# Moving projection cover from stick-breaking attention into the gated delta rule, with value transposes inside the l2 norm

## The reference

```python
(q_sb, k_sb, v_sb, q_dn, k_dn, v_dn, z_dn, b_dn, a_dn, r_sb, r_dn) = jnp.split(u @ w_in, offsets, axis=-1)
y_sb = stick_breaking_attention(rms(q_sb), rms(k_sb), v_sb) @ w_up_sb        # 8 heads x 64
qkv = silu(causal_depthwise_conv(concat([q_dn, k_dn, v_dn]), w_conv))        # 4 taps, 12 chunks of 128 channels
q_b, k_b = l2_norm(q), l2_norm(k)                                            # per head, 128 wide
o = gated_delta_rule_chunked(q_b, k_b, v_b, g, beta)                         # 4 heads x 128, a triangular solve per chunk
y_dn = (rms_norm(o, g_dn_out) * silu(z_dn)) @ w_up_dn
merged = sigmoid(r_sb) * y_sb + sigmoid(r_dn) * y_dn
```

## Time and profile before

| | |
|---|---|
| median of 3 runs | 1314.07 us (1313.59 to 1314.76) |
| the profiled execution | 1316.56 us, span 1314.8 us |
| TensorE busy | 1261.0 us, 96% of the span |
| VectorE, ScalarE, GpSimd busy | 646.7, 604.9, 61.9 us |
| mean granted TensorE clock | 0.986 of full speed |
| chain that ended last | TensorE 87%, ScalarE 5%, VectorE 4% |

### The profile page before, as it was taken

One profiled execution on the slowest core, in us unless ns is written; L12 is line 12 of the kernel. 1 busy time (PEld: TensorE's weight loads), 2 busy tenths in 40 slices (PEclk: granted clock), 3 DMA queues, 4 the chain that ended last, 5 costly groups with the idle time before them and its releaser, 6 DMA issues.

```text
span 1314.8 us, 18145 instructions
## 1 busy us (share of the span) xinstructions
PE 1261.0 (96%) x6637; PEld 1012.2 (77%) x6637; DVE 646.7 (49%) x927; ACT 604.9 (46%) x1101; POOL 61.9 (5%) x96
## 2 busy tenths in 40 slices
PE   6999999999997999999988999999799999999998
PEld 4778888887775777777767788787578888888887
DVE  4566666664445463665466366563533333332221
ACT  5476666664444455555664434553332222222211
POOL 0000000001110000000202021002000000000000
PEclk8999999999998999999989999999899999999999
DMA  9676777775652233222222110553133333333330
GB/s 312 188 199 183 191 191 191 188 206 149 163 150 56 64 80 81 65 64 81 81 57 65 50 49 26 160 176 96 49 96 96 96 96 98 98 116 109 104 89 25
DMA packets 278036, 152.38 MB, mean 116 GB/s; under 512 B 8005, under 2 KB 273374, under 8 KB 277982
## 3 DMA queue, kind: packets, MB, share of 16 engines
q1 hardware_dynamic: 273758, 149.54, 40.8%
q10 hardware_dynamic: 4224, 2.10, 0.5%
HBM read 145.31 MB, written 6.29 MB: 115 GB/s over the span
## 4 chain that ended last, share of the span: by engine, by line
PE 87%; ACT 5%; DVE 4%; issue 1%; DMA 1%; SPq 0%; ACTq 0%; DVEq 0%
PE tail L1416 12%; PE region L1416 12%; PE region L1417 12%; PE region L1418 12%; PE tail L1418 12%; PE tail L1417 12%; ACT ada_raw L582 2%; PE region L1628 2%; PE region L1434 1%; ACT w_hi L562 1%; PE region L1543 1%; PE region L1614 1%; PE region L1663 1%; PE region L1692 1%; DMA ada_early<-in_w_ada 1%
## 5 line engine op out<-in xcount | busy, mean ns | idle before, releaser
L562 ACT ACTIVATE w_hi<-raw 128x1024 fp32r<-128x1024 f32 (+1 forms) x177 | 197.7, 1117 | 519.6 <-PE tail L1418 275.8
L953 DVE TENSOR_TENSOR w_lo<-raw,w_hi 128x1024 fp32r<-128x1024 f32 (+1 forms) x177 | 229.5, 1297 | 276.2 <-ACT w_hi L562 274.6
L1416 PE MATMUL region<-u_hi,w_hi 128*128 128x512 f32 x656 | 259.2, 395 | 2.6 <-DVE w_lo L953 2.5
L1418 PE MATMUL region<-u_hi,w_lo 128*128 128x512 f32 x656 | 255.4, 389 | 0.0
L1417 PE MATMUL region<-u_lo,w_hi 128*128 128x512 f32 x656 | 255.4, 389 | 0.0
L1416 PEld LDWEIGHTS region<-u_hi,w_hi 128*128 128x128 f32 x656 | 123.1, 188 | 31.4 <-issue 5.0
L1416 PE MATMUL tail<-u_hi,w_hi 128*128 128x512 f32 x344 | 144.4, 420 | 1.9 <-DVE w_lo L953 1.9
L1417 PEld LDWEIGHTS region<-u_lo,w_hi 128*128 128x128 f32 x656 | 123.1, 188 | 27.6 <-issue 2.2
L1418 PEld LDWEIGHTS region<-u_hi,w_lo 128*128 128x128 f32 x656 | 123.1, 188 | 25.5
L1416 PE MATMUL tail<-g_hi,w_hi 128*128 128x512 f32 x352 | 141.7, 403 | 0.0
L1418 PE MATMUL tail<-g_hi,w_lo 128*128 128x512 f32 x352 | 139.2, 395 | 0.0
(11 more groups left out here) (307 smaller groups left out, 1484.6 us busy)
## 6 DMA issues: line engine op xcount, KB each, us to landing
raw<-in_w_ffn_in SPq DMA_DIRECT2D x168, 256.0 KB, 3.3
ada_raw<-in_w_ada SPq DMA_DIRECT2D x56, 512.0 KB, 5.1
raw<-in_w_in SPq DMA_DIRECT2D x90, 256.0 KB, 3.3
raw<-in_w_ffn_out SPq DMA_DIRECT2D x32, 384.0 KB, 4.6
raw<-in_w_ffn_out SPq DMA_DIRECT2D x32, 320.0 KB, 4.0
ada_early<-in_w_ada SPq DMA_DIRECT2D x8, 1024.0 KB, 9.5
gates<-kept_gates SPq DMA_DIRECT2D x16, 256.0 KB, 4.2
raw<-in_w_out SPq DMA_DIRECT2D x16, 256.0 KB, 3.3
```

What stands on the lines that cost most here:

```text
L562: act.activation(w_hi[:, slot % 2, 0:k, :], raw[:, slot, 0:k, :], ACT.Copy).then_inc(hi_ready, 1)
L953: dve.tensor_tensor(w_lo[:, slot % 2, 0:k, :], raw[:, slot, 0:k, :], w_hi[:, slot % 2, 0:k, :].bitcast(f32), ALU.subtract).then_inc(lo_rea ...
L1416: pe.matmul(bank(b), wh, xh, start=start and n == 0, stop=False)
L1418: ins = pe.matmul(bank(b), wl, xh, start=False, stop=stop and n == k - 1)
```

## The change

The order of `MIXED` becomes: ba, twelve conv, four z, sixteen gate. Attention takes three units for each pair and not four. The cover counts change to match: attention gives up 8 chunks for each pair, "silu" (the first l2 round) has 12 chunks, later rounds 8, "prep" 10 and "solved" 5. The first two squares and the first step of cover come ahead of the Silu of v and of the table load in ScalarE's queue. The transposes of v move behind the statistics of rounds 1 and 2, their copies behind the exponentials of those rounds. The four transposes of k go to four PSUM banks in place of two, without a wait for the copies.

```diff
-    + [m for h in range(4) for m in (("conv", 5 + h), ("gate", h))] + [("z", h) for h in range(4)] \
-    + [("gate", g) for g in range(4, 16)]
+    + [("conv", 5 + h) for h in range(4)] + [("z", h) for h in range(4)] + [("gate", g) for g in range(16)]
-FILL_0 = Z_0 + 4
+FILL_0 = Z_0 + 1
-SHADOW = {"keep": 20, "weights": 6, "y": 6}
-FILL = {"l2": 8, "start": 8, "prep": 7, "inv0": 2, "norm": 4, "level": 2, "join": 1, "solve": 2, "solved": 2, "step": 1, "last": 2}
+SHADOW = {"keep": 18, "weights": 3, "y": 3}
+FILL = {"silu": 12, "l2": 8, "start": 8, "prep": 10, "inv0": 2, "norm": 4, "level": 2, "join": 1, "solve": 2, "solved": 5, "step": 1,
+        "last": 2}
-    return PAIR_0 + 4 * p + n
+    return PAIR_0 + 3 * p + n
-            return gate_out if g >= DNH and g % 2 else rstd
+            return gate_out if g % 2 else rstd
# ScalarE, attention
-                mixed(pair_unit(p, 2))
                 act.wait_ge(y_ps, p + 1)
                 act.activation(ysb_hi[:, p, :], region[0][:, 0:S], ACT.Copy).then_inc(y_hi_ready, 1)
-                mixed(pair_unit(p, 3))
+                mixed(pair_unit(p, 2))
# ScalarE, l2 norm
-            act.activation(conv[:, 8:12, :], conv[:, 8:12, :], ACT.Silu).then_inc(dn_silu, 1)
-            act.preload_act_table_set("natural_log_exp_and_others")
...
                 l2_squares(m)
-                if m < DNH - 1:
-                    mixed(Z_0 + 1 + m)
-                else:
-                    fill("l2")
+                fill("l2" if m else "silu")
+                if m == 0:
+                    act.activation(conv[:, 8:12, :], conv[:, 8:12, :], ACT.Silu).then_inc(dn_silu, 1)
+                    act.preload_act_table_set("natural_log_exp_and_others")
...
+                if m in (1, 2):
+                    v_copies(range(2 * m - 2, 2 * m))
             fill("start")
-            for q in range(NB):
-                act.wait_ge(nat_ps, q + 1)
-                act.activation(v_dn[:, q], heads(bank(4 + q % 2)), ACT.Copy).then_inc(nat_v_ready, 1)
# TensorE, l2 norm
+                if m in (1, 2):
+                    v_transposes(range(2 * m - 2, 2 * m))
             fill("start")
...
+            pe.wait_ge(nat_v_ready, NB)
             pe.wait_ge(l2_ready, 8)
             for q in range(NB):
-                if q >= 2:
-                    pe.wait_ge(nat_ready, q - 1)
                 for h in range(DNH):
-                    ins = pe.transpose(bank(2 * (q % 2))[:, h * P:(h + 1) * P], conv[:, 4 + h, q * P:(q + 1) * P],
+                    ins = pe.transpose(bank((0, 2, 4, 5)[q])[:, h * P:(h + 1) * P], conv[:, 4 + h, q * P:(q + 1) * P],
                                        ident[:, :])
```

More of the change, by code:

```diff
@@ L729, in mixed @@
                 else:
-                    stored(act, d if d < DNH + 2 else d - 1)
+                    stored(act, max(d - 1, 0))
                     act.activation(gate_buffer(d)[:, :], b, ACT.Copy).then_inc(proj_ready, 1)
@@ L785, in _, with v_copies @@
                 act.activation(conv[:, L2[r], :], conv[:, L2[r], :], ACT.Silu).then_inc(dn_silu, 1)
-            act.activation(conv[:, 8:12, :], conv[:, 8:12, :], ACT.Silu).then_inc(dn_silu, 1)
-            act.preload_act_table_set("natural_log_exp_and_others")
+            def v_copies(qs):
+                for q in qs:
+                    act.wait_ge(nat_ps, q + 1)
+                    act.activation(v_dn[:, q], heads(bank(4 + q % 2)), ACT.Copy).then_inc(nat_v_ready, 1)
             def l2_squares(m):
@@ L818, in _ @@
                 act.wait_ge(nat_ps, NB + q + 1)
-                act.activation(k_dn[:, q], heads(bank(2 * (q % 2))), ACT.Copy).then_inc(nat_ready, 1)
-            act.wait_ge(proj_ready, 12 + FILL_0)
+                act.activation(k_dn[:, q], heads(bank((0, 2, 4, 5)[q])), ACT.Copy).then_inc(nat_ready, 1)
+            act.wait_ge(proj_ready, 12 + Z_0 + 4)
             act.activation(z_gate[:, :, :], z_gate[:, :, :], ACT.Silu).then_inc(z_silu, 1)
@@ L1224, in _ @@
                 mixed(pair_unit(p, 1))
-                split_lo(DN_IN + pair_unit(p, 2) + 2, 0, 0)
                 dve.wait_ge(y_hi_ready, p + 1)
@@ L1228, in _ @@
                     .then_inc(y_lo_ready, 1)
-                convolve(pair_unit(p, 2))
-                mixed(pair_unit(p, 3))
+                mixed(pair_unit(p, 2))
             fill = filler(mixed)
@@ L1682, in _, with v_transposes @@
                       start=True, stop=True).then_inc(gsum_ps, 1)
+            def v_transposes(qs):
+                pe.wait_ge(dn_silu, 9)
+                pe.wait_ge(gsum_act, 2)
+                for q in qs:
+                    if q >= 2:
+                        pe.wait_ge(nat_v_ready, q - 1)
+                    for h in range(DNH):
+                        ins = pe.transpose(bank(4 + q % 2)[:, h * P:(h + 1) * P], conv[:, 8 + h, q * P:(q + 1) * P],
+                                           ident[:, :])
+                    ins.then_inc(nat_ps, 1)
             for m in range(DNH):
[L1684 to L1687, removed]
+                fill("l2" if m else "silu")
                 for r in (2 * m, 2 * m + 1):
@@ L1692, in _ @@
                     pe.matmul(bank(r % 4), ones[:, :], work[:, r % 2, :], start=True, stop=True).then_inc(l2_stat, 1)
+                if m in (1, 2):
+                    v_transposes(range(2 * m - 2, 2 * m))
             fill("start")
-            pe.wait_ge(dn_silu, 9)
             pe.wait_ge(gsum_act, 2)
-            for q in range(NB):
-                if q >= 2:
[L1698 to L1702, removed]
+            pe.wait_ge(nat_v_ready, NB)
             pe.wait_ge(l2_ready, 8)
             for q in range(NB):
-                if q >= 2:
-                    pe.wait_ge(nat_ready, q - 1)
                 for h in range(DNH):
-                    ins = pe.transpose(bank(2 * (q % 2))[:, h * P:(h + 1) * P], conv[:, 4 + h, q * P:(q + 1) * P],
+                    ins = pe.transpose(bank((0, 2, 4, 5)[q])[:, h * P:(h + 1) * P], conv[:, 4 + h, q * P:(q + 1) * P],
                                        ident[:, :])
```

## The result

The changed kernel takes 1303.11 us (median of 4 runs, 1302.86 to 1305.43), the kernel before 1314.41 beside it; ratio 0.9915, 95% interval 0.9898 to 0.9932. That is 11.3 us less where 11.6 were forecast.

What follows compares the result with a forecast made beforehand. TensorE, busy 96% of the span, bounds the kernel; 19.6 us of waits and lost clock could be won. Gains of 7.4, 0.4, 3.2, 1.35 and 1.3 less 2.05 make 11.6, off 1314.07: 1302.5 us, range 1299 to 1306.

Steps and rivals of the forecast that it cites:

- Attention: Attention gives up 8 chunks for each pair and ends 21.8 us earlier if no wait appears.
- The spare under the exponentials: Attention, "weights" cover: three chunks last until 0.7 us after the exponentials are done.
- The l2 norm: Norm up to the k transposes: the 5.5 us gap and its 3.0 us of clock go; gain 7.4 us.
- the 2.6 us that I kept for the range: l2 norm: if Square needs its own table, two loads make VectorE start 2.6 us later; not counted in the sum.
- The sum of 9 us: Total gain if Square needs its own table, by the skill's list alone: 9 and not 11.6 us.
- the four banks: k transposes on four banks: about 2.75 us to the delta rule's first matmul where it was 3.18; gain 0.4 us.
- The delta rule: Added "prep" and "solved" chunks cover waits for dn_glast and the first v_new; shifted steps cost at three level places.
- the last scaling: End of the l2 norm: TensorE waits 1.6 us for VectorE's last scaling ahead of the k transposes.
- 3.2 + 1.35 + 1.3 - 2.05: Delta rule: prep gains 3.2 us, solved 1.35, its clock 1.3; later dn_prod copies at the levels lose 2.05.
- The first rival: New gaps let TensorE's clock fall and waits are larger; gain only 5.5 us, 1308.5 us; chance 0.2.
- The second rival: Cover worth more: rounds at 6.85 us, no level loss, no wait before k; gain 15.5, 1298.5 us; chance 0.1.
- the levels lost their 2 us: Delta rule levels: at three places the dn_prod wait goes from 0.2 to 0.9 us; loss 2.05 us.

Runs made afterwards that it cites:

- e6: Changed kernel with attention's cover (SHADOW) at keep 20, weights 1, y 3, the same 24 chunks; 1308.2 us, ratio 0.9954.
- e9: Changed kernel with the value transposes and copies back behind the start cover and the k transposes on two banks; 1303.0 us, ratio 0.9911.
- e5: Changed kernel with the squares and first step back behind the Silu of v and the table load; 1307.3 us, ratio 0.9947.
- e8: Changed kernel with squares and first step back behind Silu of v and table load, and "silu" at 16 chunks, not 12; 1303.5 us, ratio 0.9915.
- e1: Kernel before with only the l2 norm reordered; units, attention and cover counts as before; 1311.6 us, ratio 0.9979.
- e2: Changed kernel's units, attention and counts, with the l2 norm in its old order; 1307.8 us, ratio 0.9943.
- e7: Changed kernel with silu 16, l2 9, start 10, inv0 4, norm 3, level 3, join 3, solve 3, solved 6; 1298.5 us, ratio 0.9875.
- e3: Changed kernel with prep back at 7 and solved back at 2, the 12 chunks going to the rest; 1307.2 us, ratio 0.9941.

## Why the prediction was right, point by point

**Attention.** Forecast 21.8 us with no wait, measured 21.76 and none. The spare under the exponentials was put at 0.7; e6 shows 0.8.

**The l2 norm.** ScalarE's queue in the kernel after, to be read against the earlier trace rows:
```profile
628.87 4.28 ACT L784 ACTIVATE conv<-conv 128x512 f32<-128x512 f32 x8
633.05 1.14 ACT L796 ACTIVATE work<-conv 128x512 f32<-128x512 f32 x2
634.10 1.04 ACT L562 ACTIVATE w_hi<-raw 128x1024 fp32r<-128x1024 f32 x1
635.04 0.58 ACT L728 ACTIVATE z_gate<-tail 128x512 f32<-128x512 f32 x1
635.52 1.90 ACT L803 ACTIVATE conv<-conv 128x2048 f32<-128x2048 f32 x1
637.44 1.28 ACT L804 ACT_TABLE_LOAD   x1
638.74 1.27 ACT L809 ACTIVATE dn_link<-region,eps 128x512 f32<-128x512 f32 x2
```
No table load stands between the Silus and the squares, so Square ran under the Silu table: the 2.6 us that I kept for the range wasn't needed. The sum of 9 us by the Trainium skill's list of functions present in every set (ScalarE: Activation LUTs, "Table sets: the hidden batching unit"), which doesn't name Square, was the wrong one of the two. VectorE started at +14.9 and ended at +41.8 (forecast 15.2 and 41.9), these two rows against the earlier trace rows, with the norm's start at 625.61:
```profile
640.55 0.69 DVE L991 SCALAR_TENSOR_TENSOR dn_prod<-region,dn_link 128x512 f32<-128x512 f32 x1 [4.16 <-ACT dn_link L813]
...
666.75 0.69 DVE L1240 SCALAR_TENSOR_TENSOR conv<-conv,dn_link 128x512 f32<-128x512 f32 x1
```
The transposes of k come 41.98 us after the norm's start where they came at 46.47: 4.5 and, with four chunks more (2.7), 7.2 us against 7.4. The step behind them takes 2.84 us against 3.18, 0.34 where 0.4 was forecast for the four banks; but e9, with two banks, reaches the first matmul of the delta rule only 0.07 us later, so this term is not a gain by itself. The attribution was less good than the sum: I gave the new order and the cover no shares. e9 shows that the placement of the values does nothing, e5 that the early squares give 3.4, of which 1.7 are clock, and e8 that longer cover takes the gap away without them.

**The delta rule.** The rows that the forecast named, in the kernel after (the first two against the earlier trace rows, the third with the earlier trace rows, the last against the 2.1 of the earlier trace rows):
```profile
667.59 1.94 PE L1707 MATMUL region<-ident,conv 128*128 128x128 f32 x16 [1.86 <-DVE conv L1240]
...
688.16 0.68 PE L1779 MATMUL region<-dn_prod,dn_inv_t 64*64 64x64 f32 x16 [0.89 <-ACT dn_prod L846]
...
725.21 1.05 PE L1836 MATMUL region<-ssq,k_dn 128*128 128x128 f32 x7 [0.77 <-DVE ssq L1342]
```
v_new 0.77 us (0.75 forecast), dn_prod three times 0.89 (0.9), dn_glast 0.33 and nothing (0.2 and nothing), the last scaling 1.86 (1.6). The terms were 3.2 + 1.35 + 1.3 - 2.05 = 3.8; measured 4.0, the 19.1 us moved in less the 15.11 by which the stage grew. Two errors cancel in this: TensorE is idle 5.70 us in the stage against 8.02, so the waits gave 2.3 and not 2.5, and the clock gave 1.7 and not 1.3. The forecast took the clock's loss from a window that ends at 755.30, and the clock was still down behind it:
```profile
752.23:755.30 3.07, 3.07 (x16) 3.07 (x17) 0.69 (x1) 0.00 (x0) 0.00 (x0) 0.59 0.78 221
755.30:757.00 1.70, 1.70 (x14) 1.70 (x13) 0.16 (x1) 1.09 (x2) 0.00 (x0) 0.74 0.03 10
```
0.41 x 3.07 + 0.26 x 1.70 = 1.7 us.

**The first rival**, new gaps that lose the clock, did not come in the changed kernel, whose largest gap in the stretch is 1.86 us, but the clock fell in four runs beside it (e1, e2, e5, e8). With gaps of 1.9 to 2.8 us going either way, the 1.86 us in the changed kernel was close, and that it kept the clock may in part be luck. e8, with 1.93 us at the same place, shows what it would have cost, 2.7 us. The micro-idle rule of the Trainium skill (TensorE: Matmul & The Clock Gate, "A second HAM failure mode: psum-queue depth-cycling") is not borne out by these levels: waits of 0.89 us between short groups ran at a granted clock of 1.00 in all of them.

**The second rival**, that the cover is worth more, was wrong: VectorE's rounds took 7.08 us ((41.83 - 14.94 - 5.65) / 3) and not 6.85, the levels lost their 2 us and the wait ahead of k was 1.86. Its 1298.5 us is reached by e7, by other counts and not by what the rival had in mind.

Still open: why the time outside the stretch differs by up to 5 us from kernel to kernel. Before and after, the rows from 420 to 450 us show the clock's return as the difference, but no run moved only that. Open too is whether a given gap keeps or loses the clock from one execution of a kernel to the next, since each kernel has one profile.

## What to carry to other kernels

Cover taken from a stage where the busiest engine never waits costs nothing until the shortest cover there falls below the work beneath it; read that spare as start of the consumer less end of its input, and move the rest to where the waits are. A count of cover also sets when the helpers' steps fall due: a step on the last chunk ahead of a critical copy costs a chunk's time, so add up the counts point by point and look at each place where they reach a whole unit. Compare versions by the length of the changed stretch as well as by the total; here the total carried up to 5 us from elsewhere, and 1.3 us could not be seen in it. The stretch has its own trap: it is read from one execution, and one loss of clock in it (1.7 us here) is as large as many of the differences.

## What the runs showed of the hardware that was not expected

Gaps of nearly the same length keep or lose TensorE's clock. Kept: 2.23 us (before, at 712 us), 2.26 and 2.37 (e1, in the norm), 2.34 (e3). Lost: 2.11 (before), 2.23 and 2.11 (e1), 1.93 (e8), 2.77 in both runs that had it (e2, e5). No gap below 1.9 us lost it in the stretch of any of the twelve profiled executions.

The loss doesn't grow with the gap between 2.1 and 2.8 us. The granted clock over the 5 us behind the gap is 0.66 in all five cases, a loss of 0.34 x 5 = 1.7 us; before, e1 (twice), e2 and e5:
```profile
752.23:757.23 5.00, 5.00 (x30) 5.00 (x31) 1.08 (x3) 1.09 (x2) 0.00 (x0) 0.66 0.49 139
706.74:711.74 5.00, 5.00 (x58) 3.74 (x60) 3.56 (x6) 2.56 (x6) 0.51 (x1) 0.66 0.01 3
747.89:752.89 5.00, 5.00 (x30) 5.00 (x31) 1.08 (x3) 1.09 (x2) 0.00 (x0) 0.66 0.49 138
641.32:646.32 5.00, 5.00 (x11) 2.84 (x12) 1.59 (x2) 4.08 (x7) 0.03 (x1) 0.66 0.22 57
637.81:642.81 5.00, 5.00 (x11) 2.93 (x12) 1.92 (x2) 4.42 (x8) 0.03 (x1) 0.66 0.22 49
```
It was larger in e8 (2.7 us behind 1.93) and behind the 5.5 us gap (3.0).
